# Ten gathered expert rows moved to another stage, tanh in place of exponent and reciprocal, and a first block issued in another order

## The reference, cut to what matters

```python
proj = h @ w_in[l]                          # [256, 1024] x [1024, 3476 columns]
qk  = silu(causal_conv(m_q|m_k, conv_qk))   # silu(z) = z * sigmoid(z)
y_m = sigmoid(o_pre) * rmsnorm(mlstm(qk, v, gates))        # 4 heads of 128
y_b = attention(rope(rmsnorm(b_q)), rope(rmsnorm(b_k)), b_v)          # 4 heads of 64
y_n = g0*compressed + g1*selected + g2*window, g = sigmoid(n_g)  # hidden layer: silu
x = x + concat(y_m, y_b, y_n) @ w_out[l]
x = x + square(relu(rmsnorm(x) @ w_ff1[l])) @ w_ff2[l]      # 1024 -> 4096 -> 1024
```

## Time and profile before

| | us |
|---|---|
| median of 3 runs | 3462.71 (3457.69 to 3466.74) |
| the profiled execution's own time | 3462.44 |
| its span, first to last instruction | 3460.7 |
| mean granted TensorE clock | 0.854 of 2.4 GHz |
| busy: TensorE / VectorE / ScalarE / GpSimd | 2519.7 / 2284.3 / 458.6 / 1288.7 |
| moved from and to memory | 1044.64 MB, 302 GB/s |
| chain that ended last: transfers / TensorE / VectorE | 12% / 8% / 5% of the span |

### The profile page before, as it was taken

How to read it: one execution, slowest core, us unless ns; L and a number is a source line. 1 busy time by engine, 2 the same in 40 slices (tenths; PEclk the granted TensorE clock), 3 DMA queues, 4 the chain that set the end, 5 groups by cost and what they waited for, 6 DMA issues and landing times. The chain is left out here.

```text
span 3460.7 us, 25306 instructions
## 1 busy us (share of the span) xinstructions
PE 2519.7 (73%) x7868; PEld 1413.9 (41%) x7868; DVE 2284.3 (66%) x5528; ACT 458.6 (13%) x1350; POOL 1288.7 (37%) x1082
## 2 busy tenths in 40 slices
PE   5786194499939469965466888887866768888876
PEld 2344153467434438622343334343323533334332
DVE  1449665856657776665877777777635387777775
ACT  0200001100001100000111111111112111111111
POOL 0000022745533466663653444444400053444442
PEclk8998596599969569987677999999978889999999
DMA  6664262889977389999667999999941099999996
GB/s 249 247 226 166 101 220 103 274 310 392 339 250 290 129 284 346 390 327 341 235 211 275 419 418 418 419 421 421 419 174 49 31 380 419 418 419 421 421 421 280
DMA packets 248922, 1044.64 MB, mean 302 GB/s; under 512 B 20518, under 2 KB 53398, under 8 KB 176852
## 3 DMA queue, kind: packets, MB, share of 16 engines
q0 software_dynamic: 147456, 805.37, 59.0%
q1 hardware_dynamic: 93584, 222.23, 17.4%
q10 hardware_dynamic: 7748, 15.43, 1.3%
HBM read 1040.23 MB, written 2.72 MB: 301 GB/s over the span
## 5 line engine op out<-in xcount | busy, mean ns | idle before, releaser
L1178 POOL DMA_INDIRECT sb_beside_slots<-in_peer_uv,sb_beside_chosen x512 | 599.1, 1170 | 665.6 <-issue 310.5
L1151 DVE SCALAR_TENSOR_TENSOR sb_beside_slots<-sb_beside_slots,sb_beside_H 128x1024 f32<-128x1024 f32 x256 | 312.6, 1222 | 234.8 <-DMA sb_beside_slots<-in_peer_uv,sb_beside_chosen 230.0
L1170 DVE SCALAR_TENSOR_TENSOR sb_xc<-sb_beside_slots,sb_beside_small,sb_xc 128x1024 f32<-128x1024 f32 x254 | 325.7, 1282 | 6.1 <-DMA sb_beside_slots<-in_peer_uv,sb_beside_chosen 4.3
L174 PE MATMUL psum<-sb_f_arena,sb_f_ring 128*128 128x256 f32 (+1 forms) x1344 | 297.5, 385 | 5.5 <-issue 5.5
L174 PEld LDWEIGHTS psum<-sb_f_arena,sb_f_ring 128*128 128x128 f32 (+1 forms) x1344 | 252.6, 188 | 50.7 <-issue 8.3
L174 PE MATMUL psum<-sb_f_ring,sb_f_arena 128*128 128x512 f32 (+2 forms) x448 | 191.1, 588 | 7.9 <-DVE sb_f_arena L1660 7.9
L1084 PE MATMUL psum<-sb_latents_ring,sb_latents_scores 128*128 128x512 f32 x304 | 153.0, 656 | 50.1 <-ACT sb_latents_scores L1042 35.8
L1084 PE MATMUL psum<-sb_last_ring,sb_last_scores 128*128 128x512 f32 x276 | 140.1, 658 | 52.1 <-ACT sb_last_scores L1042 52.1
L1084 PE MATMUL psum<-sb_beside_slots,sb_latents_scores 128*128 128x512 f32 x288 | 142.7, 642 | 37.3 <-ACT sb_latents_scores L1042 37.3
L1888 PE MATMUL psum<-sb_f_ring,sb_f_arena 128*128 128x512 f32 x384 | 165.1, 592 | 0.0
L935 POOL DMA_INDIRECT sb_latents_ring<-in_peer_uv,sb_latents_scores x76 | 85.4, 1124 | 134.7 <-PE psum L1084 102.6
(11 more groups left out here) (512 smaller groups left out, 4856.3 us busy)
## 6 DMA issues: line engine op xcount, KB each, us to landing
sb_f_ring<-in_w_ff SPq DMA_DIRECT2D x32, 2048.0 KB
sb_context_ring<-in_ada_w SPq DMA_DIRECT2D x24, 2048.0 KB, 9.1
sb_f_ring<-in_w_in SPq DMA_DIRECT2D x8, 2048.0 KB
sb_f_ring<-in_w_in SPq DMA_DIRECT2D x6, 1904.0 KB
sb_context_ring<-in_peer_w_q SPq DMA_DIRECT2D x8, 1024.0 KB, 8.1
sb_beside_slots<-in_peer_uv,sb_beside_chosen POOLq DMA_INDIRECT x512
sb_f_ring<-in_w_out SPq DMA_DIRECT2D x4, 2048.0 KB
sb_latents_ring<-in_peer_w_q SPq DMA_DIRECT2D x8, 1024.0 KB, 17.9
```

The costliest lines, as they stand in the source:

```text
L174: last = e.matmul(out, a, b, start=(i == 0), stop=(i == len(terms) - 1))
L1151: e.scalar_tensor_tensor(out=self.u_slot[s % 4], in0=self.u_slot[s % 4], scalar=1.0, in1=self.H[:, s // (PH * TOPK), :], op0=ALU.mult, op1 ...
L1170: e.scalar_tensor_tensor(out=acc, in0=row, scalar=wn, in1=acc, op0=ALU.mult, op1=ALU.add).then_inc(self.added, 1)
L1178: return e.indirect_dma_start(out=to, out_offset=None, in_=self.table, in_offset=bass.IndirectOffsetOnAxis(ap=at, axis=0), element_offset= ...
```

## The change

It has four parts.

1. `more(12)` in the latents' (and, without effect, the last layer's) attention becomes `more(22)`; the call behind the second feed-forward becomes 28 steps in layer 0 and 18 in layer 1. One more step stands in each layer among the attention units, so the latents' attention has two fewer at its end.
2. Every sigmoid z * 1/(1 + exp(-z)) becomes 0.5 * z * (1 + tanh(z/2)): the clamp, the addition and the reciprocal go, a fused add-and-multiply stays, and the constant 0.5 is put into a factor that is there anyway. In `experts` the gelu goes the same way (the 0.5 is in g).
3. In `first_block` the projections' order is qk, gates, nat 0, o, v, [M, cn], nat 1, [s0, s1], nat 2 in place of qk, v, o, gates, nat 0, 1, 2, [M, cn, s0, s1]. The weights' ring loads in that order.
4. The norm of the heads is cut in two: groups 0 to 7 as soon as nat 1 is there, groups 12 to 21 as soon as nat 2 is there (groups 8 to 11 and 16, 17 are not normed). Two attention units come before the recurrent heads' division and norm, which now stand behind the compressing layer's product. GpSimd has six powers a layer in place of five (2, 16, 20, 8, 1, 2 columns; before 2, 8, 44, 1, 2).

```diff
-        more(12)
+        more(22)
...
-            e.tensor_scalar(rt["g"][:, q % 4, :], rt["ex"], rt["z"], None, ALU.mult).then_inc(*own.up())
+            e.tensor_scalar(rt["g"][:, q % 4, :], rt["ex"], rt["z"], 0.5, ALU.mult, ALU.mult).then_inc(*own.up())
...
-            e.scalar_tensor_tensor(out=z1, in0=z1, scalar=GELU_C, in1=d, op0=ALU.add, op1=ALU.mult).then_inc(*own.up())
-            e.wait_ge(*own.now)
-            e.tensor_scalar(z1, z1, -EXP_MAX, None, ALU.max).then_inc(z_ready, 1)
-            e.wait_ge(sig_ready, b + 1)
-            e.tensor_scalar(z2, z2, 1.0, None, ALU.add).then_inc(*own.up())
-            e.wait_ge(*own.now)
-            e.reciprocal(z2, z2).then_inc(*own.up())
-            e.wait_ge(*own.now)
-            e.tensor_tensor(w, w1, z2, ALU.mult).then_inc(w_ready, 1)
+            e.scalar_tensor_tensor(out=z1, in0=z1, scalar=GELU_C / 2, in1=d, op0=ALU.add, op1=ALU.mult).then_inc(z_ready, 1)
+            e.wait_ge(*own.now)
+            e.wait_ge(tanh_ready, b + 1)
+            e.scalar_tensor_tensor(out=w, in0=z2, scalar=1.0, in1=w1, op0=ALU.add, op1=ALU.mult).then_inc(w_ready, 1)
...
-            e.activation(z2, z1, ACT.Exp, scale=-1.0).then_inc(sig_ready, 1)
+            e.activation(z2, z1, ACT.Tanh).then_inc(tanh_ready, 1)
...
+    order = ["cols", ("hT", 0), ("hT", 1)] + [("qk", i) for i in range(4)] + ["gate", ("nat", 0), "o", "v", "M", "cn", ("nat", 1), "s0", "s1", ("nat", 2)]
+    order += [("QT", 0), ("QT", 1), ("QT", 5), ("as", 0), ("as", 1), "cmp", ("mo", 0), ("mo", 1), ("ap", 0), ("QT", 4), ("QT", 2), ("QT", 3), "kv", ("ap", 1),
+              ("ao", 0), ("as", 2), "kcT", ("ao", 1), ("as", 3), "csc", ("ap", 2), ("as", 4), "pcT", ("ap", 3), ("ao", 2), "cy", ("as", 5), ("ap", 4),
+              ("ao", 3), ("ap", 5), ("ao", 4), ("ao", 5)]
...
-        e.tensor_scalar(sig, sig, 1.0, None, ALU.add).then_inc(*own.up())
-        e.wait_ge(*own.now)
-        e.reciprocal(sig, sig).then_inc(*own.up())
-        e.wait_ge(*own.now)
-        e.tensor_tensor(qkf, qkf, sig, ALU.mult).then_inc(qk_ready, 1)
...
+        e.wait_ge(tanh_ready, 1)
+        e.scalar_tensor_tensor(out=qkf, in0=sig, scalar=1.0, in1=qkf, op0=ALU.add, op1=ALU.mult).then_inc(qk_ready, 1)
...
+        def squared_heads(g0, g1, turn):
+            r = rs3[:, :, g0:g1]
+            squares = sq[:, :].rearrange("p (t n) -> p t n", t=NT)[:, :, g0 * HD:g1 * HD]
+            e.wait_ge(qk_ready, 1)
+            e.wait_ge(*own.now)
+            e.tensor_tensor(squares, N[:, :, g0 * HD:g1 * HD], N[:, :, g0 * HD:g1 * HD], ALU.mult).then_inc(*own.up())
+            e.wait_ge(*own.now)
+            e.tensor_reduce(r, sqh[:, :, g0:g1, :], AX, ALU.add).then_inc(*own.up())
+            e.wait_ge(*own.now)
+            rms_rows(e, r, r, HD).then_inc(var, 1)
+            beside.mark((l, turn))
...
         scores(0)
+        compressed()
+        scores(1)
+        normed_heads(12, NG, 12, ((8, 4, 12, 2), (16, 4, 12, 2), (12, 2, 18, 4), (14, 2, 20, 5)), 2, qb_ready)
         beside.vector(e, 1)
         e.wait_ge(*st.emptied("cmp"))
+        e.scalar_tensor_tensor(out=hid, in0=sg, scalar=1.0, in1=hid, op0=ALU.add, op1=ALU.mult).then_inc(*own.up())
+        e.wait_ge(*own.now)
+        e.tensor_scalar(hid, hid, 0.5, None, ALU.mult).then_inc(hid_ready, 1)
+        recurrent()
+        e.wait_ge(gt_ready, 1)
+        e.tensor_scalar(gt, gt, 1.0, 0.5, ALU.add, ALU.mult).then_inc(*own.up())
+        dens(0)
+        dens(1)
         beside.vector(e, 1)
+        recurrent_out()
         beside.vector(e, 1)
         e.wait_ge(*st.computed("kv"))
...
-        beside.vector(e, 28)
+        beside.vector(e, 28 if l == 0 else 18)
```

More of the change, by code:

```diff
@@ L1405, in norm_to_T @@
             rms_rows(e, rs_, ss, D).then_inc(var, 1)
-            beside.mark((l, 0 if turn == 1 else 4))
-            e.wait_ge(rstd, turn if turn == 1 else 5)
+            beside.mark((l, 0 if turn == 1 else 5))
+            e.wait_ge(rstd, 1 if turn == 1 else 6)
             for t in range(NT):
@@ L1502, in vector @@
-        e.wait_ge(*own.now)
-        e.tensor_reduce(rs, sq[:, :].rearrange("p (g d) -> p g d", d=HD), AX, ALU.add).then_inc(*own.up())
-        e.wait_ge(*own.now)
-        rms_rows(e, rs, rs, HD).then_inc(var, 1)
-        beside.mark((l, 2))
+        e.scalar_tensor_tensor(out=W1[:, :, :], in0=st.pair("s1")[:, 0, :].rearrange("p (h n) -> p h n", h=MH), scalar=0.25 * MD ** -0.5, in1=W1[:, :, :], op0=ALU.mult, op1=ALU.mult).then_inc(*st.empties("s1"))
+        normed_heads(0, 8, 0, ((0, 4, 0, 0), (4, 4, 4, 1)), 1, qa_ready)
@@ L1507, in vector @@
+        e.wait_ge(*st.emptied(("nat", 2)))
         for c in range(2):
             for t in range(NT):
[L1509 to L1513 removed]
@@ new lines, in recurrent @@
+        def recurrent():
+            e.wait_ge(em_ready, 1)
+            for t in range(NT):
+                view = st.pair(("mo", t))[:, :, 0:2 * (MD + 1)].rearrange("p b (j c) -> p b j c", j=2)
+                d4 = dn[:, t, :].rearrange("p (b j) -> p b j", b=2)
+                e.wait_ge(*st.computed(("mo", t)))
+                e.scalar_tensor_tensor(out=d4, in0=view[:, :, :, MD], scalar=-1.0, in1=em[:, t, :].rearrange("p (b j) -> p b j", b=2), op0=ALU.mult, op1=ALU.max).then_inc(*own.up())
+                e.wait_ge(*own.now)
+                e.tensor_tensor(d4, view[:, :, :, MD], d4, ALU.max).then_inc(*own.up())
+                e.wait_ge(*own.now)
+                e.reciprocal(d4, d4).then_inc(*own.up())
+                e.wait_ge(*own.now)
+                e.tensor_tensor(mix[:, t, 0:MW].rearrange("p (b j d) -> p b j d", b=2, j=2), view[:, :, :, 0:MD], wide(d4, [P, 2, 2, MD], 3), ALU.mult).then_inc(*st.empties(("mo", t)))
+            for t in range(NT):
+                e.wait_ge(*st.emptied(("mo", t)))
+            e.tensor_tensor(sq[:, 0:NT * MW].rearrange("p (t n) -> p t n", t=NT), mix[:, :, 0:MW], mix[:, :, 0:MW], ALU.mult).then_inc(*own.up())
+            e.wait_ge(*own.now)
+            e.tensor_reduce(ssm, sq[:, 0:NT * MW].rearrange("p (g d) -> p g d", d=MD), AX, ALU.add).then_inc(*own.up())
+            e.wait_ge(*own.now)
+            rms_rows(e, ssm, ssm, MD).then_inc(var, 1)
+            beside.mark((l, 3))
@@ new lines, in recurrent_out @@
+        def recurrent_out():
+            e.wait_ge(rstd, 4)
+            e.tensor_scalar(ssm, ssm, 0.5, None, ALU.mult).then_inc(*own.up())
+            e.wait_ge(*own.now)
+            e.tensor_tensor(m4, m4, wide(ssm.rearrange("p (t h) -> p t h", t=NT), [P, NT, MH, MD], 3), ALU.mult).then_inc(*own.up())
+            e.wait_ge(*own.now)
+            e.wait_ge(*st.emptied("o"))
+            e.scalar_tensor_tensor(out=mix[:, :, 0:MW], in0=og[:, :, :], scalar=1.0, in1=mix[:, :, 0:MW], op0=ALU.add, op1=ALU.mult).then_inc(y_ready, 1)
@@ L1623, in vector @@
         dens(2)
+        beside.vector(e, 2)
+        scores(4)
         beside.vector(e, 1)
-        heads_out(1)
-        beside.vector(e, 2)
         e.wait_ge(p_exp, 1)
@@ L1761, in tensor, with heads_turned, recurrent @@
         done.then_inc(st.mm, 1)
-        for t in range(NT):
+        e.wait_ge(*landed(("nat", 2)))
+        natural(("nat", 2), weights_of(("nat", 2)), 0, 476)
+        def heads_turned(q):
+            ps = claim(("QT", q))
+            for b in range(2):
+                for t in range(NT):
+                    done = flip(e, ps[:, b, t * P:(t + 1) * P], QN[:, t, 4 * q + 2 * b:4 * q + 2 * b + 2, :].rearrange("p s d -> p (s d)"), ident)
+            done.then_inc(st.mm, 1)
+        e.wait_ge(qa_ready, NT)
+        heads_turned(0)
+        heads_turned(1)
+        e.wait_ge(qc_ready, 4)
+        heads_turned(5)
+        def recurrent(t):
             ps = claim(("mo", t))
@@ L1782, in scores @@
             s_of = flat(claim(("as", i)), "p b (h n) -> p (b h) n", h=2)[:, :, 0:nk]
-            for q in range(6) if i == 0 else ():
+            for q in {0: (0, 1), 2: (2, 3)}.get(i, ()):
                 e.wait_ge(*st.emptied(("QT", q)))
@@ L1804, in out @@
             done.then_inc(st.mm, 1)
+        scores(0)
+        scores(1)
         w = weights_of("cmp")
@@ L1812, in tensor @@
         done.then_inc(st.mm, 1)
-        scores(0)
-        scores(1)
+        recurrent(0)
+        recurrent(1)
+        p_turned(0)
+        e.wait_ge(qb_ready, NT)
+        for q in (4, 2, 3):
+            heads_turned(q)
         ps = claim("kv")
@@ L1819, in tensor @@
         done.then_inc(st.mm, 1)
-        p_turned(0)
+        p_turned(1)
+        out(0)
         scores(2)
@@ L1835, in tensor @@
         p_turned(2)
-        out(1)
         scores(4)
@@ L1843, in tensor @@
         p_turned(3)
+        out(2)
         ps = claim("cy")
```

241 lines of the change are left out of this document (97 added, 144 removed).

## The result

| | before | changed |
|---|---|---|
| median | 3462.15 us of 4 runs | 3415.27 us of 4 runs (3409.66 to 3419.62) |
| ratio, 95% interval | | 0.9864 [0.9843, 0.9884] |
| profiled execution, span | 3462.44, 3460.7 | 3419.62, 3417.8 |

The changed kernel is 1.4% faster: 47 us between the medians, 42.9 between the two profiled spans. 3425 was forecast.

What follows compares the result with a forecast made beforehand. Bounds: gathers in the experts, TensorE or VectorE by stretch in the first network. From 3462.4: -19.1 -19.1 (order), -26.9 (layer 1's tail), +31.7 (ten steps), -2.4 (two dots absent), -1.5 (tanh) = 3425 us; range 3404 to 3446.

Steps and rivals of the forecast that it cites:

- The order: Both layers, first projection to mixT: reordered projections and split head norm save 19.1 us a layer (bounds 10 to 29).
- The estimate for M, cn, s0 and s1 among the projections: Projections of each layer: these products, moved in among them, make nat 2 end 9.0 us later.
- The wait for a gather behind the third power: Before the copy of kv: the step behind `recurrent_out` waits for its row, as a gather takes 7.6 us.
- Rival C: Stretch before kv: head start kept whole, no wait behind powers, cmp shorter; -29 us a layer, 3405 us; chance 0.08.
- Tanh: First block: nothing alone, hidden under projections, but room for VectorE before M; experts: -1.5 us in all; no added table loads.
- The tail of layer 1: Behind the second feed-forward's last product: with 18 steps TensorE ends last, so the stage ends 26.9 us earlier.
- The tail of layer 0: VectorE's steps behind layer 0's last product: 28 steps kept, so its 32.4 us stay.
- The ten steps: Latents' attention: ten more steps at 3.75 us, less a wait of 5.8, cost +31.7 us (+19 to +34).
- Rival A: Units' stretch and latents' attention: the stream of rows becomes the bound, steps cost 4.0 us; 3470 us, slower; chance 0.06.
- B: Latents' attention: the moved steps are cheap, 2.5 us each, +19.2 us in place of +31.7; 3412 us; chance 0.10.
- E: Tanh is not in exp's table: each table change costs 1.28 us, 10 us a layer; 3435 us; chance 0.03.
- D: First network: only half the head start arrives, by one more wait of 9 us a layer; 3443 us; chance 0.13.

Runs made afterwards that it cites:

- the second profile: The changed kernel itself run and profiled again, nothing altered, timed against the kernel before: 3414.58 us, ratio 0.9853 [0.9825, 0.9881].

## Why the prediction was right, point by point

**The order** was worth what was forecast (-18.4 and -17.8 against -19.1 a layer, first product to mixT; -23.4 and -20.3 in the second profile), partly by luck, as its errors have opposite signs. The estimate for M, cn, s0 and s1 among the projections was 9.0 us; they took 2.0 + 0.35 + 1.9 + 1.05 = 5.3, because I took durations at the granted clock of 0.50 for products that now run at 1.00. The two pairs of windows above show it: a product moved from behind a pause to behind a busy TensorE takes half as long. The Trainium skill, "TensorE: Matmul & The Clock Gate", section "Part 1: The HAM clock gate", says as much, that the share of clock pulses let through follows how busy TensorE has recently been; for these four the trace agrees, and by that rule this term would have been 3.7 us a layer lower. The wait for a gather behind the third power was 0.8 us, not some 5: issued at 573.30 its row was there 4.3 us later, where I had taken 7.6 from a stretch with memory at a share of 0.96 (0.56 here). Against these stood VectorE's waits of 4.05 for the tanh of hid and 1.25 and 2.07 for mo. They come from the clock too: I took cmp at its old 10.56, and it took 13.80 (started at 546.97 as the walk had it, 546.8, it ended at 560.8 and not at 557.4), and mo took 5.1 in place of 2.9, at 0.50 throughout. Rival C's reason, a shorter cmp, has the wrong sign. The other side is the new wait of 4.04 for unit 1's output behind kcT, in both layers, and steps of 3.8 us in place of 3.6 (84.0/22 and 76.0/21): +8.0 and +9.2 for +5.1. And the 12 groups "squared for nothing" are 8: the powers over 16 and 20 columns replace one over 44, so groups 16 and 17 are squared still.

**Tanh** alone gives nothing: shown in the old order for the two large sigmoids, and in the new one for the experts. That it makes room for M among the projections was only argued; no kernel had the new order with reciprocals. Two table loads a layer stay, as forecast, and each takes 1.28 us:

```profile
481.71 1.28 ACT L1327 ACT_TABLE_LOAD   x1
...
483.44 1.28 ACT L1329 ACT_TABLE_LOAD   x1
```

Tanh stands ahead of them and behind, exponents too, and no load was added: by the rule that I quoted from "ScalarE: Activation LUTs" (the Trainium skill), the trace agrees.

**The tail of layer 1** went as forecast, to a tenth (-26.9). The tail of layer 0 was to stay 32.4 and is 25.4; in the changed kernel's relatives with 28 steps there it is 23.6, 26.6, 26.7, 28.0, 28.2 and 30.2, in the old order 29.4, 32.4 and 33.1. Some 4 or 5 us of the 7 may belong to the new order. VectorE has 6 to 8 dots left there when TensorE ends, and had 8 or 9; why it is further stays open.

**The ten steps** cost 33.9 in place of 31.7 (4.0 us each, not 3.75, less 5.8 of wait; bounds 19 to 34). With the tail, -26.9 + 33.9 = +7.0 would have been a loss. What makes the move neutral is the term that the prediction didn't have: -7.2 between the stages, since a stage is left only some 9 us behind GpSimd's last gather, and with steps in the tail that gather comes late. In the kernel before, where layer 1 ends (the additions end at 1558.89):

```profile
1554.61 1.69 POOL L1178 DMA_INDIRECT sb_beside_slots<-in_peer_uv,sb_beside_chosen  x1 [0.20 <-issue]
1565.90 0.30 ACTq L324 DMA_DIRECT2D sb_latents_crow<-in_c  x1
```

Rival A fell (rows don't bound the units' stretch: a step costs 2.0 us there), B too (4.0 each, not 2.5), and E (no load was added). But the argument that I set against B, that four slots and 7.6 us of landing allow one step in 3.6, doesn't follow: 7.6/4 is 1.9, or 2.5 with the step's own 2.5 us added to the 7.6. C's 29 us a layer are reached at kv in the second profile (31.2 and 30.2) and lost again by mixT; D's loss of half didn't come.

The result lies 10 us below the forecast by the medians and 5.6 by the profiled spans, as that execution of the changed kernel was the slowest of its four. In the spans two terms that I had set to nothing, the stage's end and layer 0's tail, gave 14.2, and the feed-forwards 1.3. The start of the context, untouched by the change, took 2.8 back, the order 2.0, the ten steps 2.2 and the experts and what follows 2.9. So 3425 was close because the parts were read from their own stretches, and inside that also because errors cancelled.

## What to carry to other kernels

Filler work has a price by place: here one and the same step costs 0 under the projections (up to twelve in layer 0 and six in layer 1; with eight in layer 1 TensorE waited), 2.0 us between units, 3.7 behind the last product and 4.0 beside 512-column projections, so measure a place by what the stretch becomes without the filler before moving any. An instruction removed under another engine's full stretch gave nothing by itself. Price a product by the clock that it will have in its new place: here M, cn, s0 and s1 took 3.7 us less than I had priced them at, and cmp and mo 5.4 more than they had before. Count a stage's end from the last gather that is issued, not from the last that is needed.
